# A two-layer mixer and mixture-of-experts block on one core: expert weights loaded as 16 KB runs of DRAM per partition, with turns and gathering products reading every eighth or fourth column

## The reference, cut to what matters

```
hg = jnp.einsum('btd,edf->btef', h, w_gate)
hu = jnp.einsum('btd,edf->btef', h, w_up)
act = jax.nn.silu(hg) * hu * combine[..., None].astype(h.dtype)
return jnp.einsum('btef,efd->btd', act, w_down)
```

## Time and profile before

| | |
|---|---|
| median of the runs shown | 739.67 us |
| the runs | 735.71, 739.67, 740.04 us |
| span of the profiled execution, first to last instruction | 735.1 us |
| its own time | not listed apart; the run nearest to its span is 735.71 us, 0.6 us above it |
| TensorE busy | 682.8 us, 93% |
| VectorE busy | 575.1 us, 78% |
| ScalarE busy | 433.0 us, 59% |
| moved by DMA | 220.07 MB, mean 299 GB/s |

### The profile page before, as it was taken

The page is one execution under the profiler, slowest core; times in us unless marked ns, Lnnn a source line. Parts: engine busy times, 40 slices in busy tenths (PEclk is TensorE's granted clock), DMA queues, the critical chain, the costliest instruction groups (busy, mean ns, idle before and its releaser), DMA issues.

```text
span 735.1 us, 12593 instructions
## 1 busy us (share of the span) xinstructions
PE 682.8 (93%) x4850; PEld 550.1 (75%) x4850; DVE 575.1 (78%) x838; ACT 433.0 (59%) x605; POOL 57.0 (8%) x88
## 2 busy tenths in 40 slices
PE   4699999999899999999997999999999999999981
PEld 2587998898689899954457878888888888888740
DVE  2639998898994367675398998999999999999775
ACT  1637866363232455650034579888888888888731
POOL 2060000000011010132000500000000000000220
PEclk9699999999999999999998999999999999999996
DMA  9989596645767699989626799999999999999242
GB/s 334 387 234 326 192 344 233 226 144 196 279 233 257 210 389 361 333 298 292 202 75 229 290 399 399 398 400 398 400 398 400 398 400 399 399 398 398 76 169 86
DMA packets 91508, 220.07 MB, mean 299 GB/s; under 512 B 3335, under 2 KB 3631, under 8 KB 91455
## 3 DMA queue, kind: packets, MB, share of 16 engines
q1 hardware_dynamic: 85200, 200.29, 74.2%
q0 software_dynamic: 5840, 18.94, 7.6%
q10 hardware_dynamic: 415, 0.14, 0.1%
HBM read 179.99 MB, written 39.36 MB: 298 GB/s over the span
## 4 chain that ended last, share of the span: by engine, by line
PE 73%; DVE 17%; DMA 3%; ACT 3%; issue 2%; SPq 1%; DVEq 0%; ACTq 0%
PE ps L1175 70%; DMA ring<-in_w_in 3%; PE ps L1593 2%; DVE w_lo L1756 2%; DVE arena L1911 1%; DVE arena L1910 1%; PE ps L1612 1%; DVE arena L1856 1%; DVE w_lo L2217 1%; ACT w_hi L829 1%; DVE arena L2103 1%; DVE arena L2084 1%; DVE arena L2311 1%; DVE arena L2313 1%; DVE arena L2109 1%
## 5 line engine op out<-in xcount | busy, mean ns | idle before, releaser
L2217 DVE TENSOR_TENSOR w_lo<-arena,w_hi 128x1024 fp32r<-128x1024 f32 x96 | 114.6, 1220 | 8.6 <-ACT w_hi L1059 7.4
L2217 DVE TENSOR_TENSOR w_lo<-ring,w_hi 128x1024 fp32r<-128x1024 f32 x92 | 109.9, 1220 | 8.9 <-ACT w_hi L1059 8.0
L1059 ACT ACTIVATE w_hi<-arena 128x1024 fp32r<-128x1024 f32 x96 | 101.0, 1064 | 14.9 <-PE ps L1175 14.7
L1059 ACT ACTIVATE w_hi<-ring 128x1024 fp32r<-128x1024 f32 x92 | 96.8, 1063 | 19.7 <-PE ps L1175 19.3
L1175 PE MATMUL ps<-h_hi,w_lo 128*128 128x384 f32 x288 | 101.5, 352 | 7.3 <-DVE w_lo L1756 5.2
L1175 PE MATMUL ps<-w_hi,slot_tokens_lo 128*128 128x512 f32 x256 | 102.7, 401 | 1.2 <-DVE w_lo L2217 1.1
L1175 PE MATMUL ps<-w_hi,slot_tokens_hi 128*128 128x512 f32 x256 | 100.2, 392 | 0.0
L1175 PE MATMUL ps<-w_lo,slot_tokens_hi 128*128 128x512 f32 x256 | 99.7, 390 | 0.0
L1175 PE MATMUL ps<-h_hi,w_hi 128*128 128x384 f32 x288 | 97.2, 338 | 0.0
L1175 PE MATMUL ps<-h_lo,w_hi 128*128 128x384 f32 x288 | 97.2, 337 | 0.0
L1756 DVE TENSOR_TENSOR w_lo<-ring,w_hi 128x1024 fp32r<-128x1024 f32 x44 | 53.6, 1225 | 22.4 <-ACT w_hi L829 21.4
(11 more groups left out here) (373 smaller groups left out, 1114.1 us busy)
## 6 DMA issues: line engine op xcount, KB each, us to landing
slot_rows<-arena SPq DMA_DIRECT2D x12, 2048.0 KB, 18.6
ring<-in_w_in SPq DMA_DIRECT2D x11, 2048.0 KB, 10.2
ring<-in_w_ada SPq DMA_DIRECT2D x10, 2048.0 KB, 8.9
ring<-in_w_up SPq DMA_DIRECT2D x8, 2048.0 KB, 14.7
arena<-in_w_up SPq DMA_DIRECT2D x8, 2048.0 KB, 14.9
ring<-in_w_down SPq DMA_DIRECT2D x8, 2048.0 KB, 10.9
arena<-in_w_gate SPq DMA_DIRECT2D x8, 2048.0 KB, 15.2
arena<-in_w_down SPq DMA_DIRECT2D x8, 2048.0 KB, 11.7
```

The source lines that it names most:

```text
L1059: act.activation(w_hi[:, at_ % 4, :], raw[:, q * QUARTER:(q + 1) * QUARTER], ACT.Copy).then_inc(S["hi_ready"], 1)
L2217: tt(w_lo[:, at_ % 4, :], raw[:, q * QUARTER:(q + 1) * QUARTER], w_hi[:, at_ % 4, :].bitcast(F32), ALU.subtract).then_inc(S["lo_dve"], 1)
```

## The change

In `expert_piece`, and in the load of expert 0's gate, the DRAM side of the weights is split as `(p k) n` where it was `(k p) n`. Partition p then holds rows 8p to 8p + 7 of gate and up (4p to 4p + 3 of down), which lie one after the other in DRAM, 16 KB in all, where it held rows p, 128 + p, 256 + p and so on, 2 KB or 4 KB each. Block k of the slot on partition p is then row 8p + k (4p + k). So that the products still match, block k of the turned tokens must be model columns k, 8 + k, 16 + k ..., and block k of the turned activation hidden columns k, 4 + k, 8 + k ...: the stationary operand of `selected` and of `turn` becomes every eighth column (`4 * half + k::KD`, KD = 8), that of `act_transpose` every fourth (`k::C`, C = 4), of the same tiles. No other line differs; shapes, counts and waits stay.

```diff
@@ expert_piece
-                src = a[names[j]][0][e].rearrange("a (k p) n -> p (a k) n", p=P)
+                src = a[names[j]][0][e].rearrange("a (p k) n -> p (a k) n", p=P)
@@ SP, expert 0's gate
-            src = a["w_gate"][0][0:1].rearrange("a (k p) n -> p (a k) n", p=P)
+            src = a["w_gate"][0][0:1].rearrange("a (p k) n -> p (a k) n", p=P)
@@ selected
-                        d0 = (4 * half + k) * P
                         for i in range(NT):
-                            last = mm(ps[:, 5 * b + half, k * P:(k + 1) * P], H2[:, i, d0:d0 + P], SEL[b][:, i, :], i == 0, i == NT - 1)
+                            last = mm(ps[:, 5 * b + half, k * P:(k + 1) * P], H2[:, i, 4 * half + k::KD], SEL[b][:, i, :], i == 0, i == NT - 1)
@@ turn
-                        last = pe.transpose(ps[:, half, k * P:(k + 1) * P], XG[b][:, (4 * half + k) * P:(4 * half + k + 1) * P], ident)
+                        last = pe.transpose(ps[:, half, k * P:(k + 1) * P], XG[b][:, 4 * half + k::KD], ident)
@@ act_transpose
-                    last = pe.transpose(ps[:, 2, k * P:(k + 1) * P], AC[:, k * P:(k + 1) * P], ident)
+                    last = pe.transpose(ps[:, 2, k * P:(k + 1) * P], AC[:, k::C], ident)
```

## The result

The changed kernel takes 748.27 us (median of 4 runs, 747.08 to 750.26) against 737.86 for the kernel before (4 runs beside it, 735.71 to 740.04). The ratio is 1.0143, 95% interval 1.0111 to 1.0176: slower by 10.4 us. The forecast was 762, which is 22.3 us above the 739.67 known then: the sign is right, the size more than double what was measured. The profiled run took 747.08 us.

A forecast was written before the change was run, and what follows sets the result against it. TensorE was taken to bound the kernel. 10.4 (`turn`) + 5.0 (`act_transpose`) + 8.5 (`selected`) = 23.9 us on the 735.1 us span gave 759.0; 762 was named between 759.6 and 763.6, range 737 to 768.

The forecast's parts named there:

- The bound, and the loads at 0: Expert stage: TensorE is the bound, DMA full but not waited for, so the new weight loads are worth 0.
- The slower-DMA rival: Expert weight loads: partitions 16 KB apart in DRAM slow DMA below 382 GB/s; 770 us and above, chance 0.04.
- DMA would be the pace at 18.4 us an expert: Expert stage: without TensorE's work, DMA would set the pace, 7.34 MB at 398 GB/s.
- First, does the load or the product set the pace there?: TensorE's three strided steps: a 128-column load occupies about 109 ns by itself, so a slower load shows at once.
- `turn`, priced at 10.4 us: Turning of tokens: seven loads of each turn show at 215 against 109 ns, 0.74 us, 14 times.
- `act_transpose`, priced at 5.0: Turning of the activation: three loads of each four show at 215 against 110 ns, 0.32 us, 16 times.
- How slow is a strided load?: Stationary loads of 128 columns at 16 or 32 bytes: 109 to 215 ns possible, 215 taken.
- DVE's pace over DVE's ratio: Strided load size: DVE's 1.68 ns a number gives 215 ns; its ratio of 1.62 would give 176 ns.
- `selected`: Gather of experts 0 and 1: 96 records at 215 ns take 20.6 us instead of 10.74, costing 8.5 us.
- free strides: Rival, all strided reads: TensorE's loads stay at 109 ns, nothing on the chain changes; 734 to 741 us, chance 0.19.
- full penalty: Likeliest case, all three strided reads: loads take 215 ns; 759 to 764 us, chance 0.60.
- half a penalty: Rival, strided reads: loads of 176 ns, or only the 32-byte step slowed; 750 to 759 us, chance 0.14.

The follow-up runs named there:

- e4: The changed kernel's loads (16 KB runs) with the kernel before's contiguous reads in all three places; output not the reference's: 737.54 us, ratio 0.999.
- the trimmed pair: Kernels before and after the change, both with two of three products of the experts' gate, up and down steps left out: 730.69 and 730.02 us.
- the trimmed kernel before: The kernel before with two of three products of the experts' gate, up and down steps left out: 730.69 us, ratio 0.9916.
- e2: The changed kernel with contiguous gathering reads and the old gate and up weight layout for experts 0 and 1: 738.66 us, ratio 1.0006.
- e5: The kernel before plus twelve groups of 17 unread TensorE instructions at various column steps ahead of the gather: 32-byte loads 241 ns at 1.2 GHz, 238 at 2.4.
- e1: The kernel before with only the gather of experts 0 and 1 strided and their gate and up weights in 16 KB runs: 748.32 us, ratio 1.0137.
- e3: The kernel before's loads (2 and 4 KB runs) with all three strided reads of the change; output not the reference's: 748.23 us, ratio 1.0134.
- e6: The kernel before with two of three products of each expert gate, up and down step left out: 730.69 us, ratio 0.9916.
- e7: The changed kernel with two of three products of each expert gate, up and down step left out: 730.02 us, ratio 0.9891.
- e9: The changed kernel with experts 0 and 1 gathered together, strided, 256 moving columns per record: 746.65 us, ratio 1.0104.
- e11: e9 with DVE's two residual rows moved from ahead of expert 0's up weights to behind expert 0's work: 747.58 us, ratio 1.0131.
- e12: The kernel before with only DVE's two residual rows moved behind expert 0's work: 741.09 us, ratio 1.0038.
- e10: The kernel before with experts 0 and 1 gathered together by contiguous reads, 256 moving columns per record: 747.78 us, ratio 1.0117.
- the joint strided one: The gather of e9, made for experts 0 and 1 together with strided reads on the changed kernel: 13.83 us.
- e8: The kernel before plus e5-like probe groups with 12 identity products between them: product loads 112 ns a record at 4 bytes, 240 at 32.

## Why the prediction was off

- **The bound, and the loads at 0.** Right. No engine waited for a weight load before or after, and e4 is within 0.3% of the kernel before. The slower-DMA rival is refuted: the trimmed pair moves 425 against 400 GB/s. That DMA would be the pace at 18.4 us an expert if TensorE's work were gone is right as well: the trimmed kernel before settles at 18.4, from 562 us on.
- **"First, does the load or the product set the pace there?"** This step failed: it took the path through the turns to be bound by their loads. I found turns at 109 ns, 16-column products at 113, and concluded that the load sets both paces. The rows are of two kinds: the one of products, whose load takes 112 ns, the other of transpositions, whose load takes 62 ns and whose own pass takes 109. Two equal paces had two causes. So `turn`, priced at 10.4 us, costs about 14 x 0.02 = 0.3 us, and `act_transpose`, priced at 5.0, about 16 x 0.03 = 0.5; e2 measures all of it at 0.3 us in the median (interval -0.7 to 1.6), and its trace shows 0.67 us over thirteen experts. 15.4 us of the forecast's 23.9 hung on this step.
- Rows of the trace of before spoke against that step. The prediction's own show load records of 140 to 141 ns in the two transposing lines and of 192 ns before the 16-column products, for the same 128 columns; the 51 ns between them are about those between 62 and 112. And another row I did not use:

```profile
L1410 PEld LDWEIGHTS ps<-small,arena x6: 135/138/139, 104.8 to 105.1; 36*128 36x128 f32 x6
```

  Six loads of 128 columns before transpositions of 36 rows start within 0.3 us, five intervals of about 60 ns.
- **"How slow is a strided load?"** The choice of DVE's pace over DVE's ratio went the right way: the strided load's time does not follow TensorE's clock, as e5 shows at both levels. The size was low: 240 ns a record instead of 215, 1.87 ns a column instead of 1.68. That DVE's figure lies near is no more than that: a transposition's load at the same step takes 0.86 ns a column.
- **`selected`.** The mechanism was right. Sized 8.5 us, it measured 10.0 in e1 (748.32 less 738.36, interval 8.4 to 11.7); the traces give 10.7 beside e2 and 11.7 beside the kernel before, whose gather ran wholly at the full clock. The latter closes: 25 ns more on each of 96 records are 2.4 us, and 0.76 us are a wait that I had not listed, 8.5 + 2.4 + 0.8 = 11.7. TensorE stood there for expert 1's first gate quarter, which DVE split behind expert 1's tokens, which waited for ACT's table load of 1.28 us. The wait isn't the stride's: e2 has it too (0.79 us), in place of the 1.13 us ahead of the first up product. DVE's residual work did find room under the longer gather, as said.
- **The case that came out.** None of the rivals was it: "free strides" in the two transposing lines, full penalty in the gather. I let one unknown decide all three terms together; with 8.5 us of gather alone the sum would have been 746.4 beside the median of 737.86. That 748.27 lies in the stated range of 737 to 768 is the width of the range and not the model: it falls between free strides (734 to 741) and half a penalty (750 to 759), where no case stood.
- The rule of two hits on a 16-byte line (the Trainium skill, Advanced Engine Details and Errata, SBUF Cachelines) agrees with the product's loads: 118 ns at 8 bytes, 233 at 16. For the transposition it does not: 120 ns already at 8 bytes, where a line is met twice. The free step of 4 fp32 (the Trainium skill, SBUF — State Buffer, Door 1: The DMA port swizzle) is not borne out for loads: 16 bytes cost 233 against 112.

## What to carry to other kernels

Before a slower load is priced, ask for each kind of instruction separately what sets its pace, and find a row in which the other half is short: a product of 16 columns shows a product's load, a transposition of 32 rows a transposition's. A stationary operand can be read at these steps for next to nothing where a full transposition or a product of 256 columns or more stands over it (0 to 24 ns left; fp32, 16 or 32 bytes), and at more than double the time under 128 fp32 columns. And a change that relieves an engine which nobody waits for shows its worth only once the bound is taken away: trim the bound and time both.

## What the runs showed of the hardware

- An fp32 product is recorded twice for each instruction (17 instructions, 34 records), and the load of each of those records takes about twice that of a transposition, contiguous (112 and 62 ns) and strided by 32 bytes (240 and 110).
- The strided load keeps its time at either clock: 241 ns at 0.50 and 238 to 240 at 1.00, while the contiguous one goes from 210 to 112. So do whole gathers: the strided one took 22.95 us with 0.50 until 401.4 us (the changed kernel) and until 406.1 (e1), the contiguous one 12.26 with 0.50 until 403.2 (e2) and 10.74 at 1.00 throughout (the kernel before).
- 64 bytes are faster than 32 for a product's load, 218 against 240 ns. Why is open.
- The granted clock was 0.50 at or just behind the gather's start in the changed kernel, e1, e2, e3, e6, e7, e9 and e11, some 10 us earlier, in the router, in the kernel before, e4 and e12, and in both places in e10. What decides this is open; the wait ahead of the gather was the same 1.12 us in the kernel before and in the changed one. It took 1.5 us of a contiguous gather (12.26 - 10.74), none of a strided one, and 2.3 us of the joint strided one (13.83 - 11.5).
- In e5 a clock of 0.50 lasted from 401.3 to 442 us while groups of 16-column products and 32-row transpositions kept TensorE's records without a gap; with 128-column identity products in e8 it was over by 403.4.
- With weights in runs of 2 and 4 KB a DMA that set the pace moved 400 GB/s; with runs of 16 KB it moved 425, and DVE was then busy for 96% of the stretch, so the limit with long runs may lie higher.
